# A state-space recurrence taken at every fourth token instead of every second, its inputs turned through DRAM

## What is computed

```
bu_re = jnp.einsum('bsgh,gph->bsgp', ug, bb_re)      # 16 inputs to 64 states, per group and token
bu_im = jnp.einsum('bsgh,gph->bsgp', ug, bb_im)
_, _, h_re, h_im = lax.associative_scan(complex_linear_combine, (a_re, a_im, bu_re, bu_im), axis=1)
y = (jnp.einsum('bsgp,ghp->bsgh', h_re, c_re) - jnp.einsum('bsgp,ghp->bsgh', h_im, c_im) + d_skip * ug)
y = jax.nn.gelu(y.reshape(bsz, seq, SSM_WIDTH))
y = y * jax.nn.sigmoid(y @ w_glu + b_glu)
```

## Time and profile before

| | |
|---|---|
| three runs | 3431.13, 3431.95 and 3437.24 us, median 3431.95 |
| profiled execution, first to last instruction | 3427.2 us (4.75 below the median; its own time is not listed) |
| PE, DVE, ACT, POOL busy | 3265.9 (95%), 2748.0 (80%), 1432.8 (42%), 1023.9 us (30%) |
| mean granted clock of PE | 0.986 of 2.4 GHz |
| layer 1's mixer | starts about 1702.6 us ahead of layer 2's, same pattern |

### The profile page before, as it was taken

One profiled execution on the slowest core, in us unless ns is written; L12 is line 12 of the kernel. 1 busy time (PEld: TensorE's weight loads), 2 busy tenths in 40 slices (PEclk: granted clock), 3 DMA queues, 4 the chain that ended last, 5 costly groups with the idle time before them and its releaser, 6 DMA issues. The chain is left out here.

```text
span 3427.2 us, 58447 instructions
## 1 busy us (share of the span) xinstructions
PE 3265.9 (95%) x20434; PEld 1987.8 (58%) x20434; DVE 2748.0 (80%) x5208; ACT 1432.8 (42%) x2069; POOL 1023.9 (30%) x754
## 2 busy tenths in 40 slices
PE   7998999999999899999899889999999998999996
PEld 3554756566666566666445546655656665666663
DVE  6774457898999688888858654588989997888887
ACT  5434534443444343333444445334444443333333
POOL 2410000233314444444334000003323144444443
PEclk9999999999999999999999999999999999999998
DMA  5001322689898999999540023138898989999995
GB/s 195 29 1 56 130 68 105 242 282 346 300 332 274 400 393 396 395 399 367 211 158 19 1 74 122 64 111 285 270 361 280 343 278 402 397 386 394 397 369 187
DMA packets 387132, 841.29 MB, mean 245 GB/s; under 512 B 33440, under 2 KB 232096, under 8 KB 386208
## 3 DMA queue, kind: packets, MB, share of 16 engines
q1 hardware_dynamic: 312672, 565.65, 46.1%
q0 software_dynamic: 73728, 268.47, 21.8%
q10 hardware_dynamic: 576, 5.37, 0.4%
HBM read 732.40 MB, written 106.95 MB: 245 GB/s over the span
## 5 line engine op out<-in xcount | busy, mean ns | idle before, releaser
L98 ACT ACTIVATE wh<-wf 128x1024 f16<-128x1024 f32 x656 | 690.6, 1053 | 934.0 <-PE ps L2026 491.7
L127 PE MATMUL ps<-xh,wh 128*128 128x384 f16 (+2 forms) x3008 | 1010.2, 336 | 74.0 <-DVEq L1200 36.6
L129 PE MATMUL ps<-xh,wl 128*128 128x384 f16 (+2 forms) x3008 | 1009.9, 336 | 0.0
L128 PE MATMUL ps<-xl,wh 128*128 128x384 f16 (+2 forms) x3008 | 1009.7, 336 | 0.0
L104 DVE SCALAR_TENSOR_TENSOR wl<-wf,wh 128x1024 f16<-128x1024 f32 x656 | 801.7, 1223 | 252.8 <-ACT wh L98 236.3
L2024 PE MATMUL ps<-work,wh 128*128 128x384 f16 x2048 | 667.7, 326 | 5.8 <-DVE work L2355 4.1
L2026 PE MATMUL ps<-work,wl 128*128 128x384 f16 x2048 | 667.6, 326 | 0.0
L2025 PE MATMUL ps<-work,wh 128*128 128x384 f16 x2048 | 667.6, 326 | 0.0
L2141 POOL DMA_INDIRECT xT<-urows,small x256 | 390.8, 1527 | 898.7 <-DVE xT L2223 643.5
L2149 POOL DMA_INDIRECT work<-experts,small x256 | 443.5, 1732 | 563.4 <-DVE work L2364 553.9
L127 PEld LDWEIGHTS ps<-xh,wh 128*128 128x128 f16 x3008 | 296.0, 98 | 297.3 <-DVEq L1200 37.4
(11 more groups left out here) (404 smaller groups left out, 3915.4 us busy)
## 6 DMA issues: line engine op xcount, KB each, us to landing
wf<-experts SPq DMA_DIRECT2D x512, 512.0 KB, 7.2
wf<-proj SPq DMA_DIRECT2D x144, 512.0 KB, 3.3
gates<-work SPq DMA_DIRECT2D x96, 512.0 KB, 8.0
work<-hid SPq DMA_DIRECT2D x256, 192.0 KB, 5.3
work<-gates SPq DMA_DIRECT2D x256, 192.0 KB, 6.5
hid<-work SPq DMA_DIRECT2D x192, 192.0 KB, 5.4
hid<-small SPq DMA_DIRECT2D x64, 192.0 KB, 4.9
xsave<-xT ACTq DMA_DIRECT2D x2, 2048.0 KB, 6.5
```

Source lines behind the costliest of these rows:

```text
L98: m.nc.scalar.activation(m.wh[:, slot, :], m.wf[:, k, :], ACT.Copy, scale=WS).then_inc(m.high_done, 1)
L127: m.nc.tensor.matmul(out, wh[:, k, :], xh[:, k, 0:n], start=(k == order[0]), stop=False)
L128: m.nc.tensor.matmul(out, wh[:, k, :], xl[:, k, 0:n], start=False, stop=False)
L129: last = m.nc.tensor.matmul(out, wl[:, k, :], xh[:, k, 0:n], start=False, stop=(k == order[-1]))
```

## The change

The recurrence is taken at every fourth token (`STRIDE = 4`). The inputs of four tokens stand in 128 rows of one tile (4 tokens by 32 channels), by 128 columns (`NS`), so one product of 128 rows by 128 columns gives a state tile's inputs. Two state tiles of 128 columns form a unit (`UW` = 256 columns, `UNITS` = 6), on which DVE works as it did on one tile. The output product has 128 rows (4 tokens by 32 channels): C a^o on the previous state, for o = 1 to 4, plus a direct product of the inputs with a block Toeplitz weight (C a^k B below the diagonal).

To bring four tokens into rows, the 3 input tiles are written to DRAM and read back by 12 DMAs; the outputs take the same way back before Gelu. The weights are all made on the chip: B a^1 to B a^3, turned by PE, and C a^1 to C a^4; `bz` and its load are gone, the parameter `ssm_d` is laid out anew. The rotation's angle is that of four steps, and the coarse table has 8 columns in place of 16.

The expert layer uses one set of semaphores for both gathers, with one more wait between them. The core of the diff:

```diff
+STRIDE = 4
+NS = SEQ // STRIDE
+UNITS = ST // 2
+UW = 2 * NS
...
+            if n == T_U + 11:
+                for j in range(GROUPS):
+                    sp.wait_ge(m.evac, T_U + j + 1)
+                    sp.dma_start(m.u_turn[j], u[:, j, :]).then_inc(m.moved_out, 16)
+            if n == T_U + 15:
+                sp.wait_ge(m.moved_out, 16 * GROUPS)
+                sp.wait_ge(m.prepared, 2)
+                for j in range(GROUPS):
+                    back = m.u_turn[j].rearrange("(q c) (o k) -> o c q k", q=4, o=STRIDE)
+                    for o in range(STRIDE):
+                        sp.dma_start(strided(j)[32 * o:32 * o + 32, :].rearrange("c (q k) -> c q k", q=4), back[o])\
+                            .then_inc(m.moved_back, 16)
+            if n == N_IN + 2 * RING - 1:
+                for j in range(GROUPS):
+                    sp.wait_ge(m.ssm_y, j + 1)
+                    sp.dma_start(m.y_turn[j], strided(j)).then_inc(m.moved_out, 16)
...
+        def turn_powers(t):
+            if t >= 3:
+                pe.wait_ge(m.in_out, t - 2)
+            for n in range(4):
+                last = nc.tensor.transpose(cols(B[(2, 3, 7)[t % 3]], n),
...
+                    last = MM(cols(B[n % 2], 2 * z + i), in_weights(z, st), inputs_of(st), start=True, stop=True)
...
+                MM(out, direct(st), inputs_of(st), start=True, stop=False)
+                for z in range(2):
+                    state = hh[:, n % 2, z, i * NS:(i + 1) * NS - 1]
+                    last = MM(out[:, 1:NS], cc[:, z, st, :, :].rearrange("p o c -> p (o c)"), state,
+                              start=False, stop=(z == 1))
...
+        act.wait_ge(m.in_turned, 7)
+        act.wait_ge(m.zeroed, 1)
+        for q in range(4):
+            lags = B[7][32 * q:32 * q + 32, 0:GROUPS * P].rearrange("p (j n) -> p j n", j=GROUPS)
+            for o in range(STRIDE):
+                rows, n = slice(32 * o, 32 * o + 32), P - 32 * o
+                AF(direct_a.rearrange("p (j q n) -> p j q n", j=2, q=4)[rows, :, q, 32 * o:], lags[:, 0:2, 0:n], ACT.Copy)
+                last = AF(direct_b.rearrange("p (q n) -> p q n", q=4)[rows, q, 32 * o:], lags[:, 2, 0:n], ACT.Copy)
...
-            act.wait_ge(m.ssm_y, j + 1)
+            act.wait_ge(m.moved_back, 16 * STRIDE * (GROUPS + j + 1))
...
+            for i in range(2):
+                own, decay = slice(i * NS, (i + 1) * NS), v.r4[:, 2 * n + i:2 * n + i + 1].to_broadcast([P, NS])
+                last = nc.vector.tensor_tensor_scan(gg[:, z, own], decay, vv[:, z, own], 0.0, ALU.mult, ALU.add)
...
-            ssm(h * PER_HEAD)
+            ssm(h)
...
-            ssm(h * PER_HEAD + 1)
...
+        pool.wait_ge(m.dots, N_SEL)
```

More of the change, by code:

```diff
@@ L564, in ssm_lag_weights, with ssm_out_power @@
     are, aim = (x.unsqueeze(2).to_broadcast(wide) for x in (v.are, v.aim))
[L565 to L581, removed]
+    TT(t[:, 0], old[0], are, OP.mult)
+    step(TT(t[:, 1], old[1], aim, OP.mult))
+    step(TT(new[0], t[:, 0], t[:, 1], OP.subtract))
+    TT(t[:, 0], old[0], aim, OP.mult)
+    step(TT(t[:, 1], old[1], are, OP.mult))
+    step(TT(new[1], t[:, 0], t[:, 1], OP.add))
+def ssm_out_power(m, step, v, old, new):
     nc = m.nc
@@ L726, in tensor @@
             last.then_inc(m.up, 1)
+        for t in range(3):
+            turn_powers(t)
         for i in range(3):
@@ L734, in tensor @@
                start=True, stop=True).then_inc(m.up, 1)
[L735 to L742, removed]
+        pe.wait_ge(m.prepared, 3)
+        pe.wait_ge(m.in_out, 6)
         for st in range(ST):
             j, q = st // 4, st % 4
[L745 to L748, removed]
+            out = B[7][32 * q:32 * q + 32, j * P:(j + 1) * P]
+            for part, weights in ((slice(0, 32), cz), (slice(32, P), cc)):
+                for z in range(2):
+                    rhs = weights[:, z, st, :] if part.start == 0 else \
+                        weights[:, z, st, 0:STRIDE - 1, :].rearrange("p o c -> p (o c)")
+                    last = MM(out[:, part], bs[:, z, st, :], rhs, start=(z == 0), stop=(z == 1))
+        last.then_inc(m.in_turned, 1)
         def turned_queries(r):
@@ L760, in tensor, with ssm_in @@
         pe.wait_ge(m.evac, EVAC)
[L762 to L770, removed]
+        def ssm_in(n):
+            if n == 0:
+                pe.wait_ge(m.moved_back, 16 * STRIDE * GROUPS)
+            if n >= 2:
+                pe.wait_ge(m.ssm_mul, n - 1)
+            for i in range(2):
+                for z in range(2):
+                    st = 2 * n + i
+                    last = MM(cols(B[n % 2], 2 * z + i), in_weights(z, st), inputs_of(st), start=True, stop=True)
@@ L780, in ssm_out @@
                 pe.wait_ge(m.ssm_y, j - 1)
[L781 to L787, removed]
+            for i in range(2):
+                st = 2 * n + i
+                out = cols(B[2 + j % 2], st % 4)
+                MM(out, direct(st), inputs_of(st), start=True, stop=False)
+                for z in range(2):
+                    state = hh[:, n % 2, z, i * NS:(i + 1) * NS - 1]
+                    last = MM(out[:, 1:NS], cc[:, z, st, :, :].rearrange("p o c -> p (o c)"), state,
+                              start=False, stop=(z == 1))
@@ L828, in tensor @@
                 if h:
[L829 removed]
+                    ssm_out(h - 1)
                 sb_values(h)
[L831 to L832 removed]
         def mla_s(i):
@@ L869, in tensor @@
         mla_s(0)
-        ssm_out(ST_SB - PER_HEAD)
         mla_s(1)
-        ssm_in(ST_SB)
-        ssm_out(ST_SB - 1)
+        ssm_in(BH)
+        ssm_out(BH - 1)
         for i in range(len(iters)):
@@ L1000, in scalar @@
                 stick(0)
-        for i in range(14):
+        for i in range(10):
             act.wait_ge(m.up, i + 1)
```

381 lines of the change are left out of this document (221 added, 160 removed).

## The result

The changed kernel takes **3412.28 us** (median of four runs, 3410.57 to 3420.81), the kernel before 3434.59 beside it. The ratio is 0.9939, with a 95% interval of 0.9927 to 0.9951. The forecast was 3394, with a range up to 3410. So the sign and the kind of gain came as forecast and nearly half of the size did not, and the result lies just beyond the range. The profiled execution has a span of 3408.8 us, 18.4 less than before.

The account below looks back on a forecast made before the run. PE was taken as the bound, busy 95% of the span, with DVE equally full in the stick-breaking loop. 5.9 + 13.3 - 0.2 = 19.0 us a layer, 38 in two, gave 3394 us; range 3384 to 3410.

Parts of the forecast that it names:

- Softmax part: Mixer's softmax part: shorter recurrence products on PE make it 13.3 us shorter a layer, 54 us long instead of 70.
- Projections: Mixer's projections: seven power sets on DVE instead of two, DVE busy near 63 of 65 us, PE still 65.
- First turnings, direct weights and up-products: Mixer's up-projections: DVE's later queue and PE's changed work start the first corrections 1.9 us later, bounds 0.5 and 5.
- direct-weight products: Up-projections on PE: 24 products of 32 columns plus 24 of 96, taken as 3 us, 1.7 if packed better.
- clock 1.00 in the loop: Stick-breaking loop: PE's granted clock stays full, 2.4 GHz, despite about 3 us idle a head.
- rival C: Stick-breaking loop: PE's pauses halve its clock, doubling 8.2 us a head, 29 us a layer; 3451 us; chance 0.05.
- The period of the loop: Stick-breaking loop: exponentials of heads 1 to 3 come 16.5 to 16.8 us apart instead of 18.5.
- the tail: Mixer behind the softmax part: ACT and DVE read in steps of 512 bytes, costing 0.2 us, at most 2.6.
- D: Input reads: 12 DMAs take 24 us instead of 12, costing 3 us a layer; 3400 us; chance 0.04.
- B: Softmax part doesn't follow because ACT and DVE set its pace: half the gain, 3407 to 3412 us; chance 0.06.
- F: Recurrence: a unit costs two tiles' time, DVE stays full, near 3432 us; chance 0.03 with anything cancelling the gain.
- A: DVE's queue runs later than thought, delaying the loop's start; with 3 us and other losses 3408 us; chance 0.09.

## Why the prediction came out as it did

- **The gain is of the kind forecast.** Softmax part: -14.7 against -13.3. Projections: PE 65 of 65 us busy, as said. There DVE has 56 us and not 63, because some of the power sets fall behind the window. First turnings, direct weights and up-products: 0.2 us sooner instead of 1.9 later. The 48 direct-weight products (96 passes) took 2.33 us (estimate 3).
- **The step that failed** is "clock 1.00 in the loop", that is, the weighing of rival C at a chance of 0.05. The prediction saw the pause ("PE idle about 3 us a head") and its length (2.9 measured), and named its price. It then dismissed it with one row: around a pause of 2.7 us the clock stayed at 1.00. That row is one event, in another stretch of the kernel. In front of the loop's corrections the clock fell behind 2.9 us four times in four, and it fell behind pauses down to 1.45 us (1.1, with one of 2.0 shortly ahead), though not behind every one.
- **Rival C was right in its mechanism and wrong in its size.** It doubled all 8.2 us of PE's work on the loop in each head (its three terms add up to 8.4), 29 us a layer. The clock is back before the scores of the next head: of 4.6 us 7.95 are made, 3.3 a head, 10 a layer. With these taken off, the loop's 71.5 us are 61.5, and the forecast was 61.4. This one term is 20 of the 20.4 us by which the two loops missed the forecast; all the other terms together came out 7.8 us better than forecast.
- **The period of the loop was right.** 16.5 to 16.8 us was laid out, 16.6 is measured once the clock is held.
- **Of the other rivals**, D (inputs late) didn't come: the 12 reads of the turned inputs landed 2.4 us after their issue in the median, against the 12 us allowed for them (line of the DMA view below). B and F are refuted by the softmax part, and A by the first corrections, 0.2 us sooner.
- **What the chain still hid:** the table load ahead of ACT's L960 lay in the 8.9 us from exponential to logarithm and was taken over as latency. Taking the loads out was worth 24 us with the change and 9 without it.

The line on the 12 reads, with size and median us to landing:

```profile
work<-u_turn SPq DMA_DIRECT2D x12, 64.0 KB, 2.4
```

The balance of the mixers: the loop came out at +2.4 where -7.8 was forecast, 10.2 a layer and 20.4 in all. The first stretch came out 2.1 better a layer, the softmax part 1.4 and the tail 0.4, 7.8 in all. 38 less 20.4 plus 7.8 is the 25.4 that the mixers gained.

## What to carry to other kernels

When a change relieves TensorE in a loop that hands work round several engines, ask how long TensorE will now wait in one piece: here the products behind all four pauses of 2.9 us and behind ten of twelve between 1.4 and 1.8 were slow, and those were the products that everything else waited for. One lucky pause in a trace is no proof that a length is harmless: 1.76 and 1.77 us of waiting ended differently, and other pauses of 1.5 us did nothing (last section). Look for what fills the pause before looking at what stands around it: taking out a function table that was loaded twice a head gave 24 us, the change to the recurrence itself 22. Unused products of 0.12 us a pass in the rest of the pause paid for themselves with another 8.

## What the runs showed of the hardware

- In the stick-breaking loop the clock fell behind much shorter pauses than any that the earlier trace rows made one think of. Scores and corrections behind PE's pause, full speed being 4.5 to 4.9 us, over all ten profiles of the case (a wait for DVE of 0.8 us in one head left out):

| pause ahead, us | heads | of these with the clock fallen | scores and corrections there, us |
|---|---|---|---|
| none to 0.5 | 58 | 0 | |
| 1.1 | 4 | 2 | 6.25, 7.37 |
| 1.4 to 1.8 | 12 | 10 | 6.25 to 8.99 |
| 2.1 to 2.9 | 6 | 6 | 7.5 to 8.99 |

The length of the pause right ahead is not all that decides. The two heads with a fallen clock at 1.1 us had another pause of 2.0 us ahead of their values, 3.5 us earlier; the two that kept it had none. In one of the ten at 1.4 to 1.8 the clock was down before the pause began. And ahead of other products the same lengths did less: sixteen pauses of 1.45 to 1.53 us ahead of the last head's values or of the first transposes of the softmax part never lowered the clock, those of 1.93 to 1.98 ahead of values did so twice in six, those of 2.28 ahead of the last values once in six. What else decides was not tried.

- The kernel before became slower in its loops when three of five products of `ssm_out` were left out: 73.3 and 71.4 us where 69.2 were.
- A DVE operation with both inputs in SBUF went on standing still beside POOL's table building, only at another place: the mask of each head but the first (four operations of 128x128) took 1.45 us in the changed kernel and 2.25 in the one with filled pauses, where it took 0.89 in the earlier trace rows. The tables now are built right behind the unit, which the shorter loop has moved next to the mask. The mask of the last head of layer 2, and POOL beside it:

```profile
1865.86 0.42 DVE L1388 TENSOR_TENSOR sq<-sq 128x256 f32<-128x256 f32 x1
1866.44 2.25 DVE L1416 TENSOR_TENSOR work<-work,before 128x128 f32<-128x128 f32 x4 [0.16 <-ACT work L1100]
...
1866.36 0.63 POOL L1249 TENSOR_TENSOR xh<-rs,small 128x256 f32<-128x256 f32 x1 [12.30 <-DVE sq L1388]
1866.94 0.67 POOL L1250 TENSOR_TENSOR small<-rs,small 128x256 f32<-128x256 f32 x1
1867.69 0.85 POOL L1251 TENSOR_TENSOR xh<-xh,small 128x256 f32<-128x256 f32 x1
```
